# The samples' unit of expert gathers moved behind the fourth prompt tile, with its weighed sum in four strips and an end of 256-column operations

## What is computed

```python
def _peer(h, w_query, sub_keys, expert_u, expert_v):
    ...
        sv, si = lax.top_k(s, PEER_TOPK)                       # 16 of 128 keys, two halves
        ...
        best, pos = lax.top_k(cand.reshape(...), PEER_TOPK)    # 16 of 256 pairs, per token and head
        eidx = jnp.take_along_axis(cidx.reshape(...), pos, axis=-1)
        gate = jax.nn.softmax(best, axis=-1)
        u = expert_u[eidx]                                     # (tokens, 8 heads, 16, 1024)
        v = expert_v[eidx]
        act = jax.nn.gelu(jnp.einsum('td,thed->the', xb, u), approximate=False)
        return jnp.einsum('the,thed->td', (gate * act).astype(v.dtype), v)
```

## Time and profile before

| | |
|---|---|
| median of 3 runs | 1976.27 us (1974.5 to 1977.24) |
| span of the profiled execution, first to last instruction | 1976.8 us |
| PE, DVE, ACT, POOL busy | 1502.9, 1252.3, 672.8, 625.4 us |
| gathers, from the first u product to the last | 583.6 to 1962.2 us |
| last u product to the end of the span | 14.6 us |

### The profile page before, as it was taken

One profiled execution on the slowest core, in us unless ns is written; L12 is line 12 of the kernel. 1 busy time (PEld: TensorE's weight loads), 2 busy tenths in 40 slices (PEclk: granted clock), 3 DMA queues, 4 the chain that ended last, 5 costly groups with the idle time before them and its releaser, 6 DMA issues.

```text
span 1976.8 us, 23093 instructions
## 1 busy us (share of the span) xinstructions
PE 1502.9 (76%) x7810; PEld 712.3 (36%) x7810; DVE 1252.3 (63%) x2812; ACT 672.8 (34%) x1742; POOL 625.4 (32%) x594
## 2 busy tenths in 40 slices
PE   6999899999878878768887666666666676566665
PEld 2787678898753435423333111111111111000000
DVE  2067643666565664876766667766676678677654
ACT  2135443411233443643533223342232234223222
POOL 1000000000024333344444444454444445444441
PEclk9999999899989999869988765775767776766566
DMA  9543243200559999999999999999999999999996
GB/s 315 147 141 107 89 140 130 75 22 22 224 202 404 418 416 412 419 380 419 420 420 419 421 421 417 422 403 421 421 419 418 419 407 363 422 421 421 421 422 262
DMA packets 100182, 645.41 MB, mean 326 GB/s; under 512 B 11561, under 2 KB 11617, under 8 KB 32053
## 3 DMA queue, kind: packets, MB, share of 16 engines
q0 software_dynamic: 77536, 558.01, 69.1%
q1 hardware_dynamic: 22528, 85.93, 12.1%
HBM read 638.75 MB, written 6.18 MB: 326 GB/s over the span
## 4 chain that ended last, share of the span: by engine, by line
DMA 38%; PE 37%; DVE 11%; ACT 6%; issue 6%; POOL 1%; another core or an unknown queue 1%; DVEq 0%; ACTq 0%; SPq 0%; POOLq 0%
DMA arena<-in_euv,consts 36%; PE abank L813 21%; PE fsum L1364 6%; PE dbank L813 4%; DVE arena L2014 4%; PE dbank L1364 2%; ACT consts L794 1%; PE abank L1280 1%; DMA arena<-in_wstream 1%; ACT arena L457 1%; ACT small L787 1%; POOL arena L440 1%; DVE arena L1610 1%; DVE arena L1746 1%
## 5 line engine op out<-in xcount | busy, mean ns | idle before, releaser
L2014 DVE CUSTOM_DVE_ANT_0 arena<-arena 128x1024 f32<-128x1024 f32 x520 | 633.9, 1224 | 420.2 <-DMA arena<-in_euv,consts 411.0
L440 POOL DMA_INDIRECT arena<-in_euv,consts x520 | 589.8, 1134 | 777.4 <-PE fsum L1364 540.4
L1364 PE MATMUL fsum<-arena,consts 128*32 128x512 f32 x1536 | 505.5, 837 | 307.0 <-ACT consts L794 303.9
L813 PE MATMUL abank<-arena 128*128 128x256 f32 (+4 forms) x2400 | 541.8, 384 | 11.3 <-DVE arena L1610 3.9
L813 PEld LDWEIGHTS abank<-arena 128*128 128x128 f32 (+1 forms) x2400 | 404.7, 193 | 163.1 <-issue 63.1
L787 ACT ACTIVATE small<-small 128x1 f32<-128x1 f32 x520 | 104.8, 202 | 719.5 <-DVE small L2014 712.9
L1364 PEld LDWEIGHTS fsum<-arena,consts 128*32 128x32 f32 x1536 | 60.9, 124 | 686.5 <-ACT consts L794 666.0
L1364 PE MATMUL dbank<-arena,consts 128*32 128x512 f32 x512 | 157.2, 808 | 98.7 <-ACT consts L794 98.2
L457 ACT ACTIVATE arena<-abank 128x512 f32<-128x512 f32 (+5 forms) x228 | 111.3, 488 | 316.3 <-PE abank L813 298.2
L794 ACT ACTIVATE consts<-arena,small 128x32 f32<-128x32 f32 (+1 forms) x520 | 166.9, 321 | 17.8 <-ACT small L787 0.7
L813 PE MATMUL dbank<-arena 128*128 128x128 f32 (+6 forms) x784 | 117.1, 313 | 0.7 <-ACTq L620 0.7
(11 more groups left out here) (289 smaller groups left out, 1149.8 us busy)
## 6 DMA issues: line engine op xcount, KB each, us to landing
arena<-in_wstream SPq DMA_DIRECT2D x132, 512.0 KB, 4.2
arena<-in_euv,consts POOLq DMA_INDIRECT x520
arena<-in_wout SPq DMA_DIRECT2D x8, 1024.0 KB, 10.4
arena<-mod SPq DMA_DIRECT2D x7, 512.0 KB, 12.5
arena<-in_x POOLq DMA_DIRECT2D x1, 2048.0 KB, 15.0
arena<-in_sdel POOLq DMA_DIRECT2D x1, 2048.0 KB, 8.4
out_deltas<-arena POOLq DMA_DIRECT2D x1, 2048.0 KB, 6.8
out_yp<-arena SPq DMA_DIRECT2D x4, 512.0 KB
```

The lines of the kernel that those rows point to most:

```text
L440: pool.indirect_dma_start(ring[n % SLOTS], None, I["euv"], bass.IndirectOffsetOnAxis(cur[:, u % 2, c:c + 1], 0)).then_inc(ring_in[n % SLOT ...
L813: return pe.matmul(out, lhsT, rhs, start=first, stop=last)
L1364: last = pe.matmul(out[e][to:to + 32, :], S[:, n // NQ % 2, n % NQ, :], v, start=h == 0 and kk == 0, stop=h == PH - 1 and kk == 3, skip_gr ...
L2014: TTR(uh, uh, rep[j] if t < NT else h2sb, 1.0, 0.0, ALU.mult, ALU.add, dot[:, n // NQ % 2, n % NQ:n % NQ + 1]).then_inc(s.dots_done, 1)
```

## The change

1. `UNITS` and `ORDER`: the samples' unit comes last, behind tile 3. The end steps of tile 3 (one to four ticks after it) now lie in the samples' four ticks. Tile 3 now adds into `dbank`, the samples into `fsum`.
2. The samples' `S` is 128x32 and not 128x8 (the constants get 24 more columns), and their v product goes in four quarters of 256 columns, each to its own strip of 32 rows of one bank.
3. The end of the samples works on `[128, 256]` tiles, where strip `e` holds columns 256e to 256e+255 of the 8 samples. Their gain (`gq`) and residual (`xq`) are brought into that form beforehand by 8 small transfers (L1450, L1451) at the second tile, in place of one.
4. Behind the last gather: ACT loads the root's table early, squares and sums the bank (L802), PE adds the four strips (L1383), ACT takes the root (L804), DVE multiplies with the gain meanwhile (L1997), then reciprocal and multiply-add (L1999, L2000). The result is stored by four transfers, two from SP, two from ACT.

```diff
-        UNITS = [(t, h) for t in range(NT - 1) for h in range(PH)] + [(NT, 0)] + [(NT - 1, h) for h in range(PH)]
+        UNITS = [(t, h) for t in range(NT) for h in range(PH)] + [(NT, 0)]
-        ORDER = [0, 1, 2, NT, NT - 1]
+        ORDER = list(range(NT + 1))
...
-            summed(NT - 1, n)
-            root_f(NT - 1)
+            step(A(parts4[:, 4:5], parts4[:, 0:1], ACT.Sqrt))
+            act.wait_ge(ring_used[(n - 1) % SLOTS], (n - 1) // SLOTS + 1)
+            act.wait_ge(s.fr_ready, NT)
+            act.wait_ge(s.y_ready, NT)
+            A(sq, fsum[0][:, 0:256], ACT.Square, accum_out=ssx[:, 7:8]).then_inc(s.fs_ready, 1)
+            b = aring.to_read()
+            A(rstd[:, 7:8], b[:, 0:1], ACT.Sqrt, bias=eps, scale=1.0 / D).then_inc(s.fr_ready, 1)
+            act.wait_ge(s.y_ready, NT + 1)
+            for e in (2, 3):
+                act.dma_start(O["ys"][:, 256 * e:256 * e + 256], fq[32 * e:32 * e + NB, :]).then_inc(s.out_y, 16)
...
-                            last = pe.matmul(out[e][0:NB, :], S[:, n // NQ % 2, n % NQ, 0:NB], v,
-                                             start=kk == 0 and j == 0, stop=kk == 1 and j == NQ - 1, skip_group_check=True)
+                    else:
+                        for e in range(4):
+                            v = ring[n % SLOTS][:, D + 256 * e:D + 256 * e + 256]
+                            last = pe.matmul(out[0][32 * e:32 * e + 32, 0:256], weighed, v,
                                              start=kk == 0 and j == 0, stop=kk == 1 and j == NQ - 1, skip_group_check=True)
...
+            pe.wait_ge(s.fs_ready, NT + 1)
+            b = aring.to_fill()
+            for e in range(4):
+                last = pe.matmul(b[32 * e:32 * e + 32, 0:1], consts[:, C_E4:C_E4 + 32], ssx[:, 7:8],
+                                 start=True, stop=True, skip_group_check=True)
+            last.then_inc(s.aring_full, 1)
...
-                    sp.dma_start(s_g2, I["mod"][1:NCOND, 3 * D:4 * D]).then_inc(s.sg2_in, 16)
+                    for e in range(4):
+                        here = slice(256 * e, 256 * e + 256)
+                        sp.dma_start(gq[32 * e:32 * e + NB, :], I["mod"][1:NCOND, 3 * D + 256 * e:3 * D + 256 * e + 256]).then_inc(s.sg2_in, 16)
+                        sp.dma_start(xq[32 * e:32 * e + NB, :], x_t[0:NB, NT, here]).then_inc(s.sg2_in, 16)
...
+            def finish_samples():
+
+                dve.wait_ge(s.sg2_in, 8 * 16)
+                dve.wait_ge(s.fs_ready, NT + 1)
+                step(TT(fq, fsum[0][:, 0:256], gq, ALU.mult))
+                dve.wait_ge(s.fr_ready, NT + 1)
+                step(recip(rstd[:, 7:8], rstd[:, 7:8]))
+                STT(fq, fq, rstd[:, 7:8], xq, ALU.mult, ALU.add).then_inc(s.y_ready, 1)
...
-            square_sum(NT - 1)
-            finish(NT - 1)
+            finish_samples()
```

More of the change, by code:

```diff
@@ L54, in front_order @@
     return order
-C_ID, C_LE, C_GT, C_ONE, C_LVL, C_IOTA, C_P8, C_8P, C_E4 = 0, 128, 256, 384, 512, 1408, 1424, 1432, 1560
-C_W = 1592
+C_ID, C_LE, C_GT, C_ONE, C_LVL, C_IOTA, C_P8, C_8P, C_E4 = 0, 128, 256, 384, 512, 1408, 1424, 1456, 1584
+C_W = 1616
 K_CONV, K_DN, K_SINK, K_ALOG, K_DT, K_SINKS = 0, 48, 49, 57, 61, 65
@@ L114, in build @@
         adaT = sb("adaT", [P, 2 * KT, NCOND])
-        small = sb("small", [P, 360])
+        small = sb("small", [P, 352])
         bext = sb("bext", [HQ, 384])
@@ L118, in build @@
         cpo = sb("cpo", [P, CT_N, 3])
-        arena = sb("arena", [P, 49320])
+        arena = sb("arena", [P, 49304])
         ident, le, gt, ones = (consts[:, c:c + P] for c in (C_ID, C_LE, C_GT, C_ONE))
@@ L669, in summed @@
                 step(A(t1[r, 0:512], f[0][r, :], ACT.Copy))
[L670 to L674, removed]
+                step(A(t1[0:64, 512:D], f[1][64:P, :], ACT.Copy))
+                step(A(t1[64:P, 512:D], f[1][0:64, :], ACT.Copy), s.f_out)
             def turned(t):
@@ L789, in _ @@
                         act.wait_ge(ring_used[(n - 8) % SLOTS], (n - 8) // SLOTS + 1)
[L790 to L794, removed]
+                    c0 = 32 * (NQ * j + kk if t < NT else NQ * kk + j)
+                    A(S[:, q % 2, place, :], E4g[:, u % 2, c0:c0 + 32], ACT.Copy, scale=gel[:, q % 2, place:place + 1]).then_inc(s.diag_ready, 1)
                     n += 1
@@ L1359, in _ @@
                     pe.wait_ge(s.diag_ready, n + 1)
-                    for e in range(2):
-                        v = ring[n % SLOTS][:, D + 512 * e:D + 512 * e + 512]
-                        if t < NT:
+                    weighed = S[:, n // NQ % 2, n % NQ, :]
+                    if t < NT:
+                        for e in range(2):
+                            v = ring[n % SLOTS][:, D + 512 * e:D + 512 * e + 512]
                             to = 32 * ((j + 2 * e) % NQ)
-                            last = pe.matmul(out[e][to:to + 32, :], S[:, n // NQ % 2, n % NQ, :], v,
+                            last = pe.matmul(out[e][to:to + 32, :], weighed, v,
                                              start=h == 0 and kk == 0, stop=h == PH - 1 and kk == 3, skip_group_check=True)
-                        else:
-                            last = pe.matmul(out[e][0:NB, :], S[:, n // NQ % 2, n % NQ, 0:NB], v,
+                    else:
+                        for e in range(4):
+                            v = ring[n % SLOTS][:, D + 256 * e:D + 256 * e + 256]
+                            last = pe.matmul(out[0][32 * e:32 * e + 32, 0:256], weighed, v,
                                              start=kk == 0 and j == 0, stop=kk == 1 and j == NQ - 1, skip_group_check=True)
@@ L1967, in finish @@
             def finish(t):
[L1969 to L1978, removed]
+                dve.wait_ge(s.g2_in, 16)
+                dve.wait_ge(s.fr_ready, t + 1)
+                step(recip(rstd[:, 7:8], rstd[:, 7:8]))
+                step(STT(t1, t1, rstd[:, 7:8], v_g2, ALU.mult, ALU.mult))
+                TT(x_t[:, t, :], x_t[:, t, :], t1, ALU.add).then_inc(s.y_ready, 1)
+            def finish_samples():
[3 more added lines that the diff above has]
+                dve.wait_ge(s.fr_ready, NT + 1)
+                step(recip(rstd[:, 7:8], rstd[:, 7:8]))
+                STT(fq, fq, rstd[:, 7:8], xq, ALU.mult, ALU.add).then_inc(s.y_ready, 1)
             def woven(i):
@@ L2072, in constants @@
     out.append(np.broadcast_to(np.arange(TOPK), (P, TOPK)))
-    out.append(r % NB == c[:, 0:NB])
+    out.append(r % NB == c[:, 0:32])
     out.append((c % NB == r) & (r < NB))
```

16 lines of the change are left out of this document (10 added, 6 removed).

## The result

The changed kernel takes 1953.18 us in the median of 6 runs (1948.77 to 1959.97) where the kernel before takes 1976.31 (1971.68 to 1977.8, 6 runs): a ratio of 0.9891, 95% interval 0.9874 to 0.9908. The forecast was 1968.4, its range 1964.7 to 1972.3. The sign was right; 15 us of gain were not foreseen.

What follows compares the result with a forecast made beforehand. The prediction took the gather loop to be bound by the 16 transfer engines. From 1976.27 us it took off 2.6 for the dip and 5.3 for the end, other terms 0, giving 1968.4 us, range 1964.7 to 1972.3.

Steps and rivals of the forecast that it cites:

- The bound: Loop over gathers: bound by the 16 transfer engines, 2.514 us a gather whatever the other engines do.
- Smaller edits: Wider `S`, 24 more columns of constants, eight small transfers at the second tile: 0 together, at most 0.5 us.
- The dip: 32 gathers from tile 2's end, where the samples' unit lay: 84.99 us before; 2.6 us gained, bounds 0 and 4.5.
- the sister: Same stage without samples, step from tile 1 to tile 2: 32 gathers in 82.39 us, 1.9 too much.
- the whole loss goes: Rival at the end of tile 2: without samples the ring never runs dry, 4.5 gained, 1966.5 us; chance 0.08.
- The 96 gathers behind the dip: Gathers between 1702.54 and 1943.85 us: steady pace of 2.514 us each, no change counted.
- The samples' ticks at their new place: Eight gathers behind tile 3, with tile 3's end steps hidden: cost 0, ACT late by at most 0.5 us.
- The end: From the last u product's start (T) to the span's end: T+14.6 becomes T+9.35, 5.3 us gained, bounds 3.5 and 6.4.
- the landing: Arrival of the samples' last small stores at the very end: 1.9 us taken, between 1.0 and 3.6.
- Stores in series: Rival at the end: a queue's second store begins when the first has landed, T+11.8, 1970.9 us; chance 0.07.
- ACT's queue is cold: Rival at the end: ACT's first store lands only after 15.7 us, 1981.8 us, slower than before; chance 0.04.
- The dip stays: Rival at the end of tile 2: the loss belongs to that tile's end and remains, 1971.0 us; chance 0.15.

Runs made afterwards that it cites:

- lay_sbuf: Kernel before with `small` 16 unused columns wider, so the arena with the ring slots starts 64 bytes later: 1961.48 us against 1971.65, ratio 0.9937.
- ring_only: Kernel before with ring slots 0 to 4 alone 64 bytes further, at multiples of 128 bytes: ratio 1.0 to the kernel before.
- stores_sp: Changed kernel with all four stores of the samples on SP and none on ACT: 1953.63 us, ratio 0.9915 to the kernel before.
- new_oldbase: Changed kernel with the arena put back at its old address, 64 bytes earlier: 1962.84 us, ratio 0.9954 to the kernel before.
- new_base32: Changed kernel with the arena 32 bytes earlier, ring slots at 96 and 224 modulo 256: 1958.84 us, ratio 0.9951 to the kernel before.
- new_base512: Changed kernel with the arena 128 bytes earlier, slots 0 to 4 at multiples of 512 bytes: 1948.38 us, ratio 0.9873 to the kernel before.
- old_all512: Kernel before (old order and end) with all seven ring slots at multiples of 512 bytes: 1958.52 us, ratio 0.9918 to the kernel before.

## Why the prediction was wrong, point by point

- **The bound.** That transfers bound the loop was right, and it is why a packet shorter by 1% shows in full. That their pace is given "whatever the other engines do" was taken to mean that it is given at all. This is the step that failed: the steady 2.514 us a gather was carried over to a kernel whose ring slots lie elsewhere. The edit that moved the arena and nothing else of weight (`lay_sbuf`) took the 96 gathers of that pace to 239.3 us, 2.493 each, and the loop from 1378.5 to 1364.9.
- **Smaller edits.** This is the term of the sum that held the failure. The prediction put the 24 columns of constants and the narrower tile at 0, "at most 0.5 us", by counting their bytes. Their cost in bytes is nothing. What they do is move every tile behind them by 64 bytes, which brings slots 5 and 6 to multiples of 256: 8 to 12 us under the old order (0.9937 to 0.9959), 6 to 12 under the new (0.9954 against 0.9921 and 0.9891). The whole change gave 16 to 22 us by the two ratios, where 7.9 were forecast; the address is the main part of the miss.
- **The dip.** Forecast 2.6, bounds 0 and 4.5. The stretch took 84.6 to 85.0 us in six of the eight profiles under the old order (83.0 and 83.9 in `lay_sbuf` and `ring_only`) and 80.8 to 81.9 in all under the new. At equal layout that is 1 to 4 us, mostly 3; about 1 us above the pace of the gathers behind it is left, between the sister's 1.9 and the 0 of the rival "the whole loss goes". The mechanism holds, and the sister stage was a fair measure.
- **The 96 gathers behind the dip.** Forecast unchanged. At every layout the new order makes them longer: 240.9 to 241.3 us against 242.4 and 242.7 with no slot at a multiple of 256, 239.3 to 239.9 against 240.4 to 240.8 with two, 237.8 against 239.3 to 239.6 with all. That is 1.2 to 1.7 us lost that no term had, and the shorter packets hide it in the changed kernel (240.6 against 241.3). One unit's search more falls into this stretch under the new order; that this is the cause is not shown.
- **The samples' ticks at their new place.** Forecast 0. The seven last gathers take 17.4 to 17.6 us under the new order and 18.1 to 18.3 under the old in every profile: 0.8 us gained that no term had. In the kernel before, the last gather but one comes 3.42 us behind its forerunner (1956.28 to 1959.70), after it 2.82 (1940.64 to 1943.46). Why is open. The table loads in those ticks fell where forecast (the first at 1942.48 us, behind the sixth of the eight products) and delayed nothing that the rows show.
- **The end.** Forecast T+9.35, measured T+8.3. Tile 3's finish was last before the square, as said. The one term off is the landing: forecast 1.9 us behind the last issue, measured 0.9, just below the lower bound of 1.0. The page of the Trainium skill cited there ("DMA: Bandwidth & Descriptors", "Anatomy of one DMA") has 2.0 us fixed, fitted to transfers issued from GpSimd; the small stores here, from SP and ACT, landed 0.9 us behind the last issue with two on each queue and with four on SP alone.
- **Rivals.** "Stores in series" and "ACT's queue is cold" are out (`stores_sp`: 0.4 us between them and the split). "The dip stays" is out by the profile. Order and end together came to 9 us (`new_oldbase` 0.9954, `new_base32` 0.9951), forecast 7.9. That the two agree so well is in part luck: the dip gave about 3 in place of 2.6 and the end 6.3 in place of 5.3, the last gathers gave 0.8 and the 96 before them took 1.2 to 1.7.
- **The front.** 6.7 us of the first pair of profiles are scatter ahead of the loop, which goes in part with TensorE's granted clock. Who had explained the 22.6 us of two spans stretch by stretch would have explained them too.

Open: why two slots of seven give about half of the gain of all seven, and five give all of it. A gather into a slot off the multiples of 256 is not slow by itself. From 1050 us on, the packets of 309 ns or less are 19 to 32% with no slot at a multiple, 57 to 77% with two, 99% with five and 98 to 99% with seven, so two such slots in a row (5 and 6 in `new_base512`) leave no trace, and five in a row do. Packets of several gathers are in flight on an engine at once, and their records do not part cleanly by slot. Taken in order of their start, 128 to a gather, they read 315 to 317 ns for all slots in `ring_only`; in `lay_sbuf` slots 6 and 0 read 311, 1 and 5 read 313, and 2 to 4 read 314 to 317. That fits a delay that builds up over gathers off the multiples and is made good on those at them, but no run here tests it.

## What to carry to other kernels

In a loop bound by transfers, compute the address of every destination before and after an edit, also where the edit only widens a constant: what lies behind it moves. Put the buffers that large transfers fill at multiples of 256 bytes of the partition; here that gave 0.8% under the old order (`old_all512`), with no change of order or work. If not all can lie there, most may do: five of seven gave as much in the profiles. Before crediting a change with a difference of two profiles, look at the stretch ahead of the first moved instruction: what differs there, beyond what the edit does in it, is layout or chance.

## What the runs showed of the hardware that was not expected

- Indirect gathers of 8 KB a partition into SBUF ran at 421 GB/s with no slot at a multiple of 256 bytes, 424 with two of seven and 426 to 427 with five or all; packets 315.8 to 316.8, 313.2 to 314.5 and 311.4 to 312.2 ns. Offsets of 32, 64, 96, 128 and 192 were alike within 1 ns, and 512 no better than 256. The Trainium skill's "DMA: Bandwidth & Descriptors", section "How a descriptor splits into AXI transactions", says that a descriptor is cut into transactions of 256 bytes from 256-byte boundaries; by it 8 KB off such a boundary takes one transaction more than 32, which would be 3% if each took the same time (an estimate from that page's rule). The runs agree with the boundary and show less, 1.1 to 1.7% a packet, and nothing for two such slots among five on the boundary.
- The same instructions up to the first u product took 574.5 to 584.8 us, with PE's granted clock in one stretch between 0.93 and 1.00.
- Four stores of 8 KB to HBM, issued in 1.31 us on one queue, were home 0.9 us behind the last issue.
